# A gated recurrence on one core: blocks of 32 tokens inverted at once on VectorE, the inverse put into keys and values, and one activation table for logarithm and exponential

## The chip, the cores and the metric

The kernel runs on one core of one Trainium2 chip. TensorE (PE in the tables) multiplies matrices, VectorE (DVE), ScalarE (ACT) and GpSimd (POOL) do the elementwise work, SyncE (SP) issues the DMAs. TensorE results land in eight PSUM banks of 128 partitions and 512 fp32 columns. The metric is the device time of one execution in microseconds. A profiled execution shows a trace of its own.

## The reference

Two transformer blocks, one after the other, on 512 tokens of width 1024. The change touches the second block's recurrence (and, through the activation tables, every place that takes a logarithm and then an exponential). Cut to that part:

```python
def rwkv7_mix(p, w_decay_up, w0, a_up, a0, g_up, k_k, k_a, r_k, lnx_g, lnx_b):
    r, k, v, wd, ad, gd = jnp.split(p, c, axis=-1)          # p: token-shifted projections
    w = -jax.nn.softplus(-(w0 + jnp.tanh(wd) @ w_decay_up)) - 0.5
    a = jax.nn.sigmoid(a0 + ad @ a_up)
    g = jax.nn.sigmoid(gd) @ g_up
    kk = (k * k_k) / max(norm(k * k_k), 1e-12)              # per head of 64
    k = k * (1.0 + (a - 1.0) * k_a)
    decay = jnp.exp(-jnp.exp(w))
    def step(state, inp):                                    # one token, 8 heads, state 64x64
        r_t, d_t, k_t, v_t, kk_t, a_t = inp
        sa = jnp.einsum('bhij,bhj->bhi', state, -kk_t)
        state = (state * d_t[:, :, None, :]
                 + sa[..., None] * (kk_t * a_t)[:, :, None, :]
                 + v_t[..., None] * k_t[:, :, None, :])
        return state, jnp.einsum('bhij,bhj->bhi', state, r_t)
    ...                                                      # group norm, bonus, gate g
```

The second block then has index attention, two output projections, a feed-forward layer and norms; all of them keep their form. Inputs, outputs and parameters are fp32.

## The kernel before

Activations lie transposed: features on partitions, the 512 tokens along the free axis, in tiles of 128x512 numbered 0 to 49 (`tile(i)`). A weight matrix arrives in panels of 128x2048 (1 MB): SP loads one, ScalarE casts its high part (line 1129, `W<-raw`), GpSimd subtracts to get the low part (line 2133), and TensorE takes three fp32r products for each pair of tiles (lines 389 to 391, `product`). One `project` job is 24 such products with 512 columns. Two panels can be raw and two split at a time. Where a panel is split is decided by the order of the code: each engine's program calls `ahead` or `filled` with a TensorE job, and the splits that this job's end permits are put in front.

Each engine has one queue in the order of its code; semaphores tie them together (`pe_done` counts TensorE jobs, `bankN_read` the reads of a PSUM bank, others are named after what they announce). No planner orders the work.

The second block's recurrence is done in four chunks of 128 tokens (loop over `t`), each as two halves of 64 (`e`), for 8 heads of 64 features; a tile holds two heads, the two halves of its partitions. Names of products: `rm` = decayed beta times kappa, whose strict upper part M is to be inverted (I + M), `rn` = keys times kappa, `rb` and `rk` the same with the receptance (RHO), `vrow`, `brow`, `krow` are transposes, `nv` = `rn` times values.

What happens, in order:

- `project("rkv", ..., 12)` and `project("wag", ..., 2)`: 14 jobs, each read on VectorE by `causal_conv` with two taps (token shift, lines 1584 and 1586).
- Preparation, lines 1982 to 2005 on VectorE, 1432 to 1458 on ScalarE, 2245 to 2249 on GpSimd: low-rank products `wup`, `aup`, `gup` (lines 882, 885, 890), head norms `kkn` and bonus `bon` (line 443), the running sum of the logarithm of the decay (1987), its exponentials (1452 to 1455), the scaled keys.
- For each chunk: `rm` (line 911), then `inverse`: level 0 by a mask (GpSimd line 2173, VectorE line 1596), transposes (454), then five levels of doubling. A level is: mask (POOL 2173), product (467), copy (ACT 1191), two products (476, 482), two subtractions (DVE 1602, 1604). `rn`, `rb`, `rk`, `nv` and the transposes are put between (`RW_BETWEEN`, lines 902 to 911, masks on VectorE line 2012).
- For each half: state times keys (929), plus values (DVE 2027), times the inverse (938), negated copy (ACT 1465), state times receptance (945), state update (954, 955), added and decayed on VectorE (2031, 2033). At a chunk's end the output product (964, 965), added on VectorE (2038).
- Group norm (`gmean`, `gvar`, line 443; ScalarE 1473, 1178, 1181), then the `ai` projections of the index attention.

The first block's recurrence already inverts its 32-token blocks on VectorE, with `unit_inverses` (lines 1746 to 1770): transposes of 32x32 blocks (1751), a copy to PSUM (1754), 30 steps of a product and a subtraction (1760, 1761), and back (1764, 1766).

A norm's root is taken as exp(-0.5 ln x): `rstd` (lines 1163, 1164) and `rstds` (1178, 1181). `logarithm_next` (1168) takes a logarithm of no use ahead of time, so that its table is there.

## Time and profile before

| | |
|---|---|
| median of 3 runs | 2430.56 us (2429.46 to 2431.78) |
| the profiled execution's own time | 2427.37 us |
| its span | 2425.6 us |
| PE / DVE / ACT / POOL busy | 2189.3 / 960.2 / 834.9 / 929.5 us |
| chain that ended last | PE 75%, DVE 17%, ACT 4%, issue 2%, POOL 2%, DMA 1% |

The page's second part cuts the span in 40 slices of 60.6 us (a digit is the busy share in tenths, PEclk the granted TensorE clock):

```profile
PE   6986999999999889999989588889899888999997
DVE  2587449836431332221022843332892552000001
PEclk9997999999999999999999688888899999999999
```

Slices 23 to 27 (counted from 0; 1395 to 1698 us) hold the second recurrence: TensorE is not full and its clock is not fully granted. Slice 22 is the preparation before it.

### The profile page before, as it was taken

How to read it: one execution, taken by the hardware profiler on the slowest of the kernel's cores; microseconds unless marked ns; L12 is line 12 of the kernel's file. 1: busy time of each engine (PE TensorE's matmuls, PEld its weight loads, DVE VectorE, ACT ScalarE, POOL GpSimd, SP SyncE). 2: the span in 40 equal slices, each digit the busy share in tenths (PEclk: the TensorE clock that was granted, in tenths of full speed). 3: DMA queues.
4: the chain of work that ended last, by engine and by line, in shares of the span. 5: the costliest groups of instructions: out<-in, count | busy, mean ns of one | idle time of the engine just before them, and what ended most of it. 6: DMA issues, size and time to landing. Idle time of an engine off the chain costs nothing.

```text
span 2425.6 us, 28119 instructions
## 1 busy us (share of the span) xinstructions
PE 2189.3 (90%) x11186; PEld 1763.6 (73%) x11186; DVE 960.2 (40%) x1520; ACT 834.9 (34%) x1098; POOL 929.5 (38%) x350
## 2 busy tenths in 40 slices
PE   6986999999999889999989588889899888999997
PEld 3674888766778768888867278776687666888886
DVE  2587449836431332221022843332892552000001
ACT  3544243365452233222222411114322553322222
POOL 2433524433124345545534412222133224555453
PEclk9997999999999999999999688888899999999999
DMA  6121124410112322222332000000122121222231
GB/s 266 70 70 35 35 105 180 173 68 35 50 55 88 121 70 104 91 101 102 107 123 103 18 1 1 1 1 35 53 73 101 37 103 70 87 104 87 104 105 69
DMA packets 25328, 194.36 MB, mean 80 GB/s; under 512 B 3056, under 2 KB 3312, under 8 KB 4208
## 3 DMA queue, kind: packets, MB, share of 16 engines
q1 hardware_dynamic: 25200, 192.57, 21.9%
q8 instruction: 90, 1.47, 0.2%
q14 instruction: 38, 0.31, 0.0%
HBM read 188.37 MB, written 4.19 MB: 79 GB/s over the span
## 4 chain that ended last, share of the span: by engine, by line
PE 75%; DVE 17%; ACT 4%; issue 2%; POOL 2%; DMA 1%; DVEq 0%; SPq 0%; ACTq 0%; POOLq 0%
PE ps L389 19%; PE ps L390 19%; PE ps L391 18%; PE ps L443 2%; PE ps L476 2%; DVE st L1623 1%; PE ps L467 1%; DVE ar L2072 1%; PE ps L911 1%; PE ps L482 1%; POOL W L2133 1%; DVE sm L2071 1%; ACT W L1129 1%; PE ps L512 1%; DVE ar L1567 1%
## 5 line engine op out<-in xcount | busy, mean ns | idle before, releaser
L2133 POOL TENSOR_TENSOR W<-raw,W 128x2048 fp32r<-128x2048 f32 x146 | 673.8, 4615 | 1117.4 <-ACT W L1129 1117.0
L389 PE MATMUL ps<-hH,W 128*128 128x512 f32 x1648 | 661.0, 401 | 47.2 <-DVE arR L1578 8.0
L391 PE MATMUL ps<-hH,W 128*128 128x512 f32 x1648 | 646.6, 392 | 0.0
L390 PE MATMUL ps<-arR,W 128*128 128x512 f32 x1392 | 544.3, 391 | 0.0
L1129 ACT CAST W<-raw 128x2048 fp32r<-128x2048 f32 x146 | 278.9, 1910 | 629.3 <-PE ps L391 619.6
L389 PEld LDWEIGHTS ps<-hH,W 128*128 128x128 f32 x1648 | 312.5, 190 | 136.3 <-issue 54.0
L391 PEld LDWEIGHTS ps<-hH,W 128*128 128x128 f32 x1648 | 312.3, 189 | 66.8
L390 PE MATMUL ps<-xL,W 128*128 128x512 f32 x848 | 334.3, 394 | 0.0
L390 PEld LDWEIGHTS ps<-arR,W 128*128 128x128 f32 x1392 | 263.4, 189 | 53.7
L389 PE MATMUL ps<-arR,W 128*128 128x512 f32 x592 | 233.1, 394 | 16.1 <-DVE arR L1552 12.7
L391 PE MATMUL ps<-arR,W 128*128 128x512 f32 x592 | 232.3, 392 | 0.0
L390 PEld LDWEIGHTS ps<-xL,W 128*128 128x128 f32 x848 | 162.1, 191 | 33.1 <-issue 2.2
L389 PEld LDWEIGHTS ps<-arR,W 128*128 128x128 f32 x592 | 112.5, 190 | 41.5 <-DVE arR L1552 8.7
L2173 POOL TENSOR_TENSOR ar<-ar,cm 128x512 f32<-128x512 f32 x48 | 62.5, 1303 | 182.1 <-DVE ar L2019 108.9
L391 PEld LDWEIGHTS ps<-arR,W 128*128 128x128 f32 x592 | 112.1, 189 | 23.6
L443 PE MATMUL ps<-ar,cm 128*128 128x512 f32 x172 | 86.8, 646 | 33.0 <-DVE ar L1996 17.9
L2106 DVE TENSOR_TENSOR ar<-ar,ps 128x512 f32<-128x512 f32 x22 | 15.1, 688 | 220.6 <-PE ps L391 220.6
L1586 DVE SCALAR_TENSOR_TENSOR ar<-ps,cols,ar 128x511 f32<-128x511 f32 (+1 forms) x130 | 97.4, 749 | 4.6
L443 PEld LDWEIGHTS ps<-ar,cm 128*128 128x128 f32 x172 | 33.0, 202 | 77.8 <-issue 58.6
L1584 DVE TENSOR_SCALAR ar<-ps,cols 128x512 f32<-128x512 f32 x46 | 35.9, 779 | 103.7 <-PE ps L391 103.3
L1133 ACT CAST arR<-ar 128x512 fp32r<-128x512 f32 x74 | 46.0, 621 | 79.4 <-DVE ar L2106 29.5
L1602 DVE TENSOR_TENSOR ar<-ar,ps 128x512 f32<-128x512 f32 x40 | 27.5, 688 | 109.9 <-PE ps L482 93.2
(365 smaller groups left out, 2663.6 us busy)
## 6 DMA issues: line engine op xcount, KB each, us to landing
raw<-panels_dram SPq DMA_DIRECT2D x146, 1024.0 KB, 4.7
ar<-ada_dram SPq DMA_DIRECT2D x12, 2048.0 KB, 11.2
xT<-xT_dram SPq DMA_DIRECT2D x2, 2048.0 KB, 7.8
out_dram<-xT SPq DMA_DIRECT2D x1, 2048.0 KB, 7.3
xT<-out_dram SPq DMA_DIRECT2D x1, 2048.0 KB, 7.7
out_dram<-xT SPq DMA_DIRECT2D x4, 512.0 KB, 2.6
cm<-cm_dram SPq DMA_DIRECT2D x1, 1152.0 KB, 31.4
wide<-wide_dram SPq DMA_DIRECT2D x1, 1024.0 KB, 4.7
```

The lines of the kernel that those rows point to most:

```text
L389: mm(out, lhs[0], rhs[0], start=first, stop=False)
L390: mm(out, lhs[0], rhs[1], start=False, stop=False)
L391: return mm(out, lhs[1], rhs[0], start=False, stop=final)
L443: ins = mm(pst(name, i), sel[k] if isinstance(sel, list) else const(sel), sq, start=(k == 0), stop=(k == len(squares) - 1))
L476: ins = mm(heads4((name, "xt", t, lv, hf))[:, h, :], pair(p1, hf)[:, h, :], pair(xtr, hf)[:, h, :], start=True, stop=True)
L1129: link(nc.scalar.copy(W[:, n % SPLIT, 0, :], raw[:, n % RAW, :]), panel_high, n + 1)
L1133: link(nc.scalar.copy(dst, src), done, value)
L1584: link(ts(out, src, taps[-1], bias, ALU.mult, ALU.add if bias is not None else ALU.bypass))
L1586: ins = stt(out[:, j:S], src[:, 0:S - j], taps[n - 1 - j], out[:, j:S], ALU.mult, ALU.add)
L1602: link(tt(pair(xtr, hf), pair(xtr, hf), heads4((name, "xt", t, lv, hf)), ALU.subtract), *read((name, "xt", t, lv, hf)))
L2133: link(tt(W[:, n % SPLIT, 1, :], raw[:, n % RAW, :], W[:, n % SPLIT, 0, :].bitcast(F32), ALU.subtract), panel_low, n + 1)
L2173: link(tt(pair(mk, hf), pair(am, hf), bm(const(f"lvl{lv}")), ALU.mult), s, value)
```

## The change

One rewrite of the second recurrence and one edit of `logarithm_next`.

- The inverse. `rm` is computed for all four chunks first; one `unit_inverses` call on VectorE inverts all 32-token blocks of all heads and chunks (it now takes its tiles as arguments and serves both blocks). The step from 32 to 64 tokens stays on TensorE: `invert_0` (transposes), `invert_1` (p5), `invert_2` (xt5), for chunks 0 and 1 ahead of the loop, for 2 and 3 inside it. ScalarE copies the off-diagonal corners (`corners`), GpSimd clears them.
- Order of the projections: `wag` job 0 and keys first (`RKV_ORDER` = 12, 4..7, 0..3, 8..11, 13); six of the 14 jobs, `bon` and `gup` stand on TensorE beside the VectorE inverse. The panel of `wag` is loaded twice ("gd").
- The loop. The inverse is multiplied into keys (`solved_keys`, `xk`, scaled by the decay on VectorE) and into values (`solved_values`). The state is one 128x512 tile, two heads to a 128x128 block, so that a half is: `solved_state` (four products, added in PSUM to the solved values), a copy on ScalarE (`updates`), `state_update` (four products, added in PSUM to `key_values`), an addition and a decay on VectorE (`state`). Outputs are summed in one bank (`yt`).
- The preparation moves some VectorE products to GpSimd (keys, receptance, bonus) and to ScalarE (`kap`), and drops the scaling of the decay into the activations (`RATE`).
- `logarithm_next` preloads the table set that holds both functions; eight more calls of it stand ahead of groups of such functions.
- The `trig` load waits until the last `yt`. Banks: chain 0 to 3 for u, z and y, work 4 to 7.

```diff
-    for i in range(7):
+    for i in (5, 6):
...
+RW_U, RW_Z, RW_Y, RW_WORK = (0, 1), (2,), (3,), (4, 5, 6, 7)
+RKV_ORDER = (12, *range(4, 8), *range(4), *range(8, 12), 13)
...
-                project("rkv", h_mix, 12, lambda k: norm_step("low", "rms3", k))
-                project("wag", h_mix, 2)
+                project("wag", h_mix, 1, lambda k: norm_step("low", "rms3", k))
+                project("rkv", h_mix, 1, i0=4)
...
+                for t in range(NT):
+                    products("rm", t, ALL_BANKS)
...
+                project("rkv", h_mix, 1, i0=3, banks=CHAIN_BANKS)
+                project("rkv", h_mix, 4, i0=8, banks=CHAIN_BANKS)
+                project("gd", h_mix, 1, i0=1, banks=CHAIN_BANKS)
...
+                def solved_values(t, e):
...
+                        ins = mm(pst(("u", t, e))[eb, h * 64:(h + 1) * 64], pair(RW_AX + 2 * t, h % 2)[:, h // 2, eb], tile(NVT[t])[:, h * 64:(h + 1) * 64],
+                                 start=(h == 0), stop=(t + e == 0 and h == H - 1))
...
+                def solved_state(t, e):
...
+                    for p in range(4):
+                        ins = mm(pst(("u", t, e))[eb, p * P:(p + 1) * P], tile(KAP + p)[:, ec], tile(RW_T)[:, p * P:(p + 1) * P], start=False, stop=(p == 3))
...
+                for t in range(NT):
+                    if t:
+                        solved_state(t, 0)
+                    solved_values(t, 1)
+                    out_values(t)
+                    products("rb", t, RW_WORK)
+                    rows("brow", t, RW_WORK)
+                    if t:
+                        out_state(t, 0)
+                    key_values(t, 0)
+                    state_update(t, 0)
+                    if t + 1 < NT:
+                        products("rk", t + 1, RW_WORK)
+                    if t + 2 < NT:
+                        invert_0(t + 2)
+                    solved_state(t, 1)
+                    if t + 1 < NT:
+                        key_values(t, 1)
+                    out_state(t, 1)
+                    if t + 1 < NT:
+                        rows("krow", t + 1, RW_WORK)
+                    if t + 2 < NT:
+                        invert_1(t + 2)
+                    if t + 1 < NT:
+                        state_update(t, 1)
+                    out_update(t)
+                    if t + 2 < NT:
+                        invert_2(t + 2)
+                    if t + 1 < NT:
+                        solved_keys(t + 1)
+                        solved_values(t + 1, 0)
...
-                link(af(st[:, 60:61], col("one"), ACT.Ln))
+                nc.scalar.preload_act_table_set("natural_log_exp_and_others")
...
+                for k in range(1, 31):
+                    n = 31 - k
+                    product = tile(temporary)[:, 0:n * k].rearrange("p (i j) -> p i j", j=k)
+                    link(tt(product, low3[:, k + 1:32, k:k + 1].to_broadcast([P, n, k]), unit3[:, k:k + 1, 0:k].to_broadcast([P, n, k]), ALU.mult))
+                    link(tt(unit3[:, k + 1:32, 0:k], unit3[:, k + 1:32, 0:k], product, ALU.subtract))
...
+                units = unit_inverses(RW_AX, RW_LOW, RW_PRODUCT, "rw_blocks", "rw_solved")
+                next(units)
+                mix(8)
+                mix(9)
+                for _ in range(5):
+                    next(units)
```

VectorE where the inverse of the first chunk begins, before. Names are line, operation, output<-input, shape; 1596 makes level 0, 1602 and 1604 are a level's subtractions, 2012 a mask of `rn`:

```order
L2019 COPY ar<-ps 128x512 [waits pe_done,rw_state]
L2019 COPY ar<-ps 128x512 [waits pe_done,bank1_read]
L1596 TENSOR_TENSOR ar<-cm,ar 128x512 [waits rw_masked0,bank2_read]
L1596 TENSOR_TENSOR ar<-cm,ar 128x512 [waits rw_masked0,rw_xt0]
L1602 TENSOR_TENSOR ar<-ar,ps 128x512 [waits pe_done,rw_xt0]
L1604 TENSOR_TENSOR ar<-ar,ps 128x512 [waits bank1_read]
L1602 TENSOR_TENSOR ar<-ar,ps 128x512 [waits pe_done,bank2_read]
L1604 TENSOR_TENSOR ar<-ar,ps 128x512 [waits bank3_read]
L2012 TENSOR_TENSOR ar<-ps,cm 128x512 [waits pe_done,bank4_read]
```

The same engine and place in the changed kernel, from the last mask of `rm` (2195) on; 1790 to 1794 open `unit_inverses`, 1777 and 1779 are the token shift of a projection, 1799 and 1800 a step:

```order
L2195 TENSOR_TENSOR ar<-ps,cm 128x512 [waits pe_done,bank1_read]
L1790 STREAM_TRANSPOSE ar<-ar 32x1024 [waits bank2_read]
L1790 STREAM_TRANSPOSE ar<-ar 32x1024 [waits dve_chain] x3
L1793 TENSOR_SCALAR ps<-ar 128x512 [waits pe_done,dve_chain] x2
L1794 MEMSET ps 128x32 [waits dve_chain]
L1777 TENSOR_SCALAR ar<-ps,sm4 128x512 [waits pe_done,dve_chain]
L1779 SCALAR_TENSOR_TENSOR ar<-ps,cols,ar 128x511 [waits dve_chain]
L1777 TENSOR_SCALAR ar<-ps,sm4 128x512 [waits pe_done,bank3_read]
L1779 SCALAR_TENSOR_TENSOR ar<-ps,cols,ar 128x511 [waits dve_chain]
L1799 TENSOR_TENSOR ar<-ar,ps 128x30 [waits bank4_read]
L1800 TENSOR_TENSOR ps<-ps,ar 128x30 [waits dve_chain]
L1799 TENSOR_TENSOR ar<-ar,ps 128x58 [waits dve_chain]
```

What moved: the waits for TensorE and GpSimd inside the inverse are gone; its steps wait for VectorE itself, and projections are read between them.

TensorE in a half, before. 929 is state times keys, 938 the product with the inverse, 945 state times receptance (its second group, one more row, and then the update of lines 954 and 955 follow):

```order
L929 MATMUL ps<-ar 64x64 [waits bank3_read,rw_state]
L929 MATMUL ps<-ar 64x64 x3
L929 MATMUL ps<-ar 64x64 [waits bank4_read]
L929 MATMUL ps<-ar 64x64 x3
L938 MATMUL ps<-ar 64x64 [waits rw_rhs,bank5_read,bank2_read,bank1_read]
L938 MATMUL ps<-ar 64x64 x7
L945 MATMUL ps<-ar 64x64 [waits bank6_read]
```

And in the changed kernel, the second half of the third chunk (`t` = 2, `e` = 1); 991 is `solved_state`, 1000 `key_values`, 1026 `out_state`, 878 the transposes of the next keys, 1008 `state_update`:

```order
L991 MATMUL ps<-ar 64x128 [waits bank5_read,bank2_read]
L991 MATMUL ps<-ar 64x128 x3
L1000 MATMUL ps<-ar 128x128 [waits bank2_read,bank4_read]
L1000 MATMUL ps<-ar 128x128 x3
L1026 MATMUL ps<-ar 128x64 [waits rw_decayed]
L1026 MATMUL ps<-ar 128x64 x3
L878 MATMUL ps<-cm,ar 128x128 [waits bank7_read]
L878 MATMUL ps<-cm,ar 128x128 x3
L1008 MATMUL ps<-trig,ar 128x128 [waits bank4_read,bank1_read]
L1008 MATMUL ps<-trig,ar 128x128 x3
```

Two groups carry the state (991 and 1008) where there were three (929, 938, 954 with 955), VectorE no longer stands between the first and the second (`rw_rhs` is gone), and twelve products that wait for neither group lie between them.

ScalarE at the last norm of the program (`rstd`), before; 1168 is `logarithm_next`, 1163 the logarithm, 1164 the exponential:

```order
L1168 ACT_TABLE_LOAD
L1168 ACTIVATE st<-cols 128x1 [waits norm_squares]
L1163 ACTIVATE ar<-ps,cols 128x512 [waits pe_done,act_chain]
L1164 ACT_TABLE_LOAD
L1164 ACTIVATE ar<-ar 128x512 [waits bank2_read]
```

And in the changed kernel:

```order
L1286 ACT_TABLE_LOAD [waits norm_squares]
L1281 ACTIVATE ar<-ps,cols 128x512 [waits pe_done]
L1282 ACTIVATE ar<-ar 128x512 [waits bank0_read]
```

The table load between the two functions is gone. In the whole program ScalarE's table loads go from 56 to 35.

## Rows read from the trace of the kernel before

**Rows 1.** Busy time by stage: length, instructions, granted clock (PEclk), DMA.
```profile
1257.00:1330.00 73.00, 72.80 (x321) 60.05 (x322) 21.06 (x29) 14.51 (x11) 27.66 (x6) 1.00 0.24 84
1330.00:1387.00 57.00, 26.77 (x58) 11.94 (x56) 50.48 (x55) 28.92 (x43) 26.09 (x15) 0.68 0.06 22
1387.00:1455.00 68.00, 57.38 (x518) 53.53 (x519) 24.91 (x40) 12.01 (x22) 15.89 (x13) 0.83 0.01 1
...
1591.00:1655.00 64.00, 55.84 (x501) 52.05 (x501) 21.57 (x37) 12.01 (x22) 13.12 (x10) 0.83 0.00 1
```
**Rows 2.** Chain that ended last, 1380 to 1660 us: start, length, engine, line.
```profile
1380.81 2.09 PE ps L911 x11
...
1387.03 1.97 PE ps L454 x8
...
1454.67 1.97 PE ps L454 x8
...
1654.94 3.69 PE ps L443 x8
```
**Rows 3.** Groups by line, 1387 to 1655 us: busy us, mean ns, idle before.
```profile
L467 PE MATMUL ps<-ar 128*128 128x128 f32 x320 | 49.5, 306 | 10.6 <-DVE ar L1604 10.6
...
L2012 DVE TENSOR_TENSOR ar<-ps,cm 128x512 f32<-128x512 f32 x24 | 16.6, 692 | 0.8
```
**Rows 4.** Timeline of one half, chunk 2: start, length, operation, idle before.
```profile
1501.11 1.94 PE L938 MATMUL ps<-ar 64*64 64x64 f32 x16 [2.64 <-DVE st L1654]
...
1503.14 0.59 ACT L1465 ACTIVATE ar<-ps 64x512 f32<-64x512 f32 x1 [6.67 <-PE ps L938]
...
1505.92 0.42 DVE L2031 TENSOR_TENSOR ar<-ar,ps 128x256 f32<-128x256 f32 x1 [5.07 <-PE ps L955]
...
1509.17 1.64 PE L938 MATMUL ps<-ar 64*64 64x64 f32 x13 [0.72 <-DVE st L1654]
```
**Rows 5.** Chain of waits, 1460 to 1486 us: small products back to back.
```profile
1462.57 0.89 PE ps L482 x8
...
1484.10 1.73 PE ps L902 x16
```
**Rows 6.** Groups by line, VectorE, whole span: the first block's `unit_inverses`.
```profile
L1761 DVE TENSOR_TENSOR ps<-ps,ar 128x30 f32<-128x30 f32 (+14 forms) x30 | 10.1, 338 | 1.0
...
L1760 DVE TENSOR_TENSOR ar<-ar,ps 128x30 f32<-128x30 f32 (+14 forms) x30 | 9.8, 328 | 1.0
...
L1751 DVE STREAM_TRANSPOSE ar<-ar 32x1024 f32<-32x1024 f32 x4 | 8.2, 2044 | 0.1
...
L1766 DVE STREAM_TRANSPOSE ar<-ar 32x1024 f32<-32x1024 f32 x4 | 7.6, 1911 | 0.1
...
L1764 DVE COPY ar<-ps 128x512 f32<-128x512 f32 x2 | 1.4, 693 | 0.1
```
**Rows 7.** Timeline, preparation: token shift's first operation, an exponential.
```profile
1330.45 0.75 DVE L1584 TENSOR_SCALAR ar<-ps,sm 128x512 f32<-128x512 f32 x1 [3.90 <-PE ps L391]
...
1370.99 0.63 ACT L1452 ACTIVATE ar<-ar 128x512 f32<-128x512 f32 x1 [13.86 <-DVE ar L2002]
```
**Rows 8.** Stretches of 2 us in the halves of chunk 2.
```profile
1500.00:1502.00 2.00, 0.89 (x9) 0.92 (x10) 0.75 (x3) 0.00 (x0) 0.00 (x0) 0.60 0.00 0
...
1518.00:1520.00 2.00, 1.20 (x14) 1.01 (x13) 1.56 (x3) 0.00 (x0) 0.41 (x1) 1.00 0.00 0
```
**Rows 9.** Timeline, preparation: VectorE beside GpSimd.
```profile
1333.47 3.69 DVE L1552 TENSOR_TENSOR narrow<-wix,narrow 128x64 fp32r<-128x64 f32 x1 [1.48 <-ACT narrow L1133]
...
1351.09 1.72 POOL L2245 TENSOR_TENSOR ar<-ar 128x512 f32<-128x512 f32 x1 [14.01 <-DVE ar L1994]
...
1351.72 1.64 DVE L1996 SCALAR_TENSOR_TENSOR ar<-ar,cols 128x512 f32<-128x512 f32 x1
```
**Rows 10.** Chain of waits at the third norm.
```profile
1244.50 1.28 ACT L1164
```
**Rows 11.** Groups by line, ScalarE, whole span.
```profile
L1181 ACT ACT_TABLE_LOAD x11 | 14.1, 1283 | 0.2
```

More of the change, by code:

```diff
@@ L956, in block_2, with rows @@
-                        end(ins)
+                            ins[par] = mm(heads4((what, t, par))[:, p, :], tile(lhs + p)[b, c], tile(rhs + p)[b, c], start=True, stop=True)
+                    for par in range(2):
+                        end(ins[par], ((what, t, par), 0))
+                def rows(what, t, banks):
+                    begin((what, t), banks=banks)
+                    for p in range(4):
+                        ins = turn(heads4((what, t))[:, p, :], tile({"vrow": V2, "brow": BT, "krow": KT, "kaprow": KAP}[what] + p)[:, t * P:(t + 1) * P],
+                                   const("ident"))
+                    end(ins)
@@ new lines, in row @@
+                def row(base, t, h):
+                    return tile(base + h // 2)[:, t * P + 64 * (h % 2):t * P + 64 * (h % 2) + 64]
+                pe.wait_ge(sem("rw_ready"), 4)
+                for t in range(NT):
+                    products("rm", t, ALL_BANKS)
+                for b in range(2):
+                    begin("rw_blocks", b, (DENSE_BANKS[b],))
+                    end(mm(pst("rw_blocks", b)[:, 0:1], const("ident"), const("ones")[:, 0:1], start=True, stop=True))
+                project("rkv", h_mix, 1, i0=3, banks=CHAIN_BANKS)
@@ new lines, in later_values @@
+                def later_values(t):
+                    for par in range(2):
+                        emptied(pe, ("rn", t, par))
+                    emptied(pe, ("vrow", t))
+                    begin(("nv", t), banks=CHAIN_BANKS)
+                    for h in range(H):
+                        ins = mm(pst(("nv", t))[:, h * 64:(h + 1) * 64], pair(NTR[t % 2], h % 2)[:, h // 2, :], row(V2, t, h), start=True, stop=True)
+                    end(ins)
+                pe.wait_ge(sem("kt_ready"), 4)
@@ L1432, in block_2, with in_place @@
+                def in_place(base, t):
+                    return ar[:, base:base + 4, t * P:(t + 1) * P]
+                emptied(act, "wag", 0)
                 link(af(tile(WA)[0:64, :], tile(WA)[0:64, :], ACT.Tanh), sem("lora_act"), 1)
-                act.wait_ge(small2_in, 32)
+                key_parts(0)
+                for p in range(4):
+                    filled(act, "wup", p)
+                    link(af(tile(LD + p), pst("wup", p), ACT.Sigmoid, bias=col("w0", p)), *read("wup", p))
@@ L1440, in block_2 @@
+                logarithm_next()
+                decays(0)
+                decays(1)
+                key_parts(2)
+                decays(2)
+                decays(3)
+                key_parts(3)
                 for p in range(4):
@@ L1997, in block_2 @@
+                for _ in range(3):
+                    next(units)
+                mix(12)
+                for _ in range(3):
+                    next(units)
+                mix(13)
+                for _ in range(3):
+                    next(units)
                 for p in range(4):
```

650 lines of the change are left out of this document (376 added, 274 removed).

## The prediction, as it was put on record before the changed kernel ran

> **What bounds the kernel now.** I read the page's slices first. TensorE is busy to nine tenths nearly everywhere; the exception of length is the second recurrence. The table of stretches by stage [rows 1] shows the order of things: from 1257 to 1330 us TensorE is full at the full clock with 14 projection jobs (321 products in 72.8 us, 0.227 us each, 5.45 us a job of 24). From 1330 to 1387 VectorE is busy 50.5 of 57 us and TensorE 26.8: the preparation is bound by VectorE. Then come four chunks of about 68 us in which TensorE counts as busy 57 us, at a mean granted clock of 0.83.
>
> The chain that ended last gives the borders [rows 2]: first `rm` products at 1380.8, first transposes at 1387.0, those of the second chunk at 1454.7 (the two between repeat at 68 us), group norm at 1654.9. So from 1257.2 to 1654.9 there are 397.7 us, of which the four chunks take 267.9.
>
> Within a chunk the chain goes product, copy, two products, two subtractions, level after level; from the borders and the half below, some 46 us of the 68 are the inverse. The five levels' first product alone is 320 records, 160 products (an fp32 product leaves two) [rows 3]. A half is a chain of its own: product with the inverse at 1501.11, copy 2.03 us later, state addition at 1505.92, next half's product at 1509.17 [rows 4]: 8.06 us a half. So before, waits and dependent products set the length; TensorE's 0.89 us for four 128x128 products, 0.22 each, and 1.73 us for eight with 64 columns, again 0.22 each [rows 5], are the other price.
>
> **The change, part by part.** The old stage from 1257.2 to 1654.9 is replaced by four pieces, each worked out from rows.
>
> *a, to the last mask of `rm`.* TensorE's work up to `rw_ready` is eight jobs (43.6 us) and twelve fp32 products of 512 columns, 0.86 us each (four of 0.22; four in a row took 3.69 with their start [rows 2]): 10.3 us. The first job runs in the shadow of the norm and ends about 1.2 us after 1257.2, so without any wait TensorE is through at 1258.4 + 38.2 + 10.3 = 1307. Then a token shift (two operations of 0.75 and their starts, 1.57 [rows 7]), three multiplications, 32 products of `rm` (7 us; 3.5 if the two halves of the rows work at once), the last masks (0.69 each [rows 3]): 1315 to 1319. That is the lower end. VectorE's own share is about 43 us (eight shifts 12.6, four running sums and differences 8, twelve multiplications, four factors, four decays, four clips and eight masks 23), so it isn't the bound either; the two wait for each other and for ScalarE (16 exponentials at 0.63 [rows 7], Sigmoid, Tanh and table loads at 1.28, all in one queue, where the second `key_parts` waits for a projection before `aup` can be read). Following that queue job by job I come to `rw_ready` at 1316 without disturbance.
>
> What stands against it: VectorE beside GpSimd. A VectorE operation that takes 0.69 us alone took 1.64 while GpSimd multiplied, and a 64-column subtraction took 3.69 under a panel's split [rows 9]. The change puts eight GpSimd multiplications of 1.7 us and about four splits of 4.6 us into this piece. I take 3 us for the rest after the queue's own course and 7 for `rm` and its masks, which follow one another by bank: end at 1326. Upper end 1340, if each of the splits is met.
>
> The Trainium skill ("SBUF — State Buffer", Who interferes with whom) says that a VectorE instruction with two SBUF inputs and a GpSimd instruction that reads SBUF exclude each other for their whole length, and that one with a single SBUF input outside the two-port modes is free. The trace agrees in the 1.64 us row. By that rule alone all 8 x 1.7 + 4 x 4.6 = 32 us of GpSimd could fall on VectorE here, and nothing on the inverse, whose steps read one operand from PSUM. That is the second rival below.
>
> *b, the block inverse.* The first block runs the same code on the same shapes: 10.1 + 9.8 + 8.2 + 7.6 and twice 1.4 for copies [rows 6], and some 67 starts of 0.03: 40.6 us. Beside it in the same queue: six shifts (9.4), four bonus products (2.9), eight masks of `rn` (5.6), a small subtraction (0.3): 58.8. TensorE delivers its six jobs at 5.45 us from 1326 to 1359, which VectorE has to await for some 4 us in all (the gate's job is the last: 1359, shift to 1360.5, and 27 us of steps, masks and the final transposes remain). I take 64, so `rw_solved` at 1390. Ends 59 and 72 (the small subtraction under a split 3.7, low clock in the first jobs). The six jobs, 33 us, that stood ahead of everything now lie beside it and cost nothing.
>
> *c, before the loop.* Inverse steps of chunks 0 and 1, `rk`, `krow`, `xk`, first values: 76 products at 0.22 are 16.7, and TensorE has been idle before, so the first few microseconds run at the half clock, as at 1500 to 1502 [rows 8]. I take 20 (14 to 26): loop begins at 1410.
>
> *d, the loop.* A full chunk has 96 products and transposes (solved state 8, solved values 16, output values 8, `rb` 8, `rk` 8, transposes 8, output state 8, key values 8, update 8, output update 8, keys 8); the first has 88, the last 60, and chunks 0 and 1 carry 24 of the inverse each. That is 112 + 120 + 96 + 60 = 388, against 268 a chunk, 1072 in all, before. At 0.22 each they would be 85 us. About half are 64 wide on one side and go pairwise on the two halves of the array's columns, or load half the weights; the small products of the old half took 1.94 us for eight at a clock of 0.60 [rows 4, 8]. I take 0.173 as the mean: 67 us. The chain is shorter than this: four products 0.9, copy 0.59, four products 0.9, addition in two parts of 0.42 [rows 4], 0.4 of handing over: 3.7 us a half, 30 for eight. So the loop is bound by TensorE's order. For waits at bank turns, the unhidden last chunk and a clock that falls now and then I add 11: 78 us. Ends 66 and 92. `gmean` then starts at 1488 to 1489, against 1654.9.
>
> Pieces: 1654.9 - 1488.9 = 166.0 us saved.
>
> *Tables.* On the chain between logarithm and exponential stands a load of 1.28 us [rows 10]. It goes at four norms (5.1 us; the first norm waits for DMA anyway), at the latent norm (1.3), in the head norms of the attention (two loads in one queue, 2) and at the group norm (1.3). Of the eleven loads of line 1181 [rows 11] most are hidden by TensorE's work and give nothing. I take 10, between 6 and 15. The Tanh load that is new lies in piece a.
>
> The Trainium skill ("ScalarE: Activation LUTs", What ACT_TABLE_LOAD costs) gives about 2.66 us for each switch of set, load and drain together. The rows here show 1.28 and an exponential that starts 0.02 us later; by the page the edit would give some 20 us instead of 10.
>
> *At nothing:* the second load of the `wag` panel (one cast and one split beside VectorE's inverse), the later `trig` load (its first reader comes after five projections of 5.45 us), fewer constants. If their cover were gone, the panel would cost 1.9 + 4.6 us.
>
> **Sum.** The profiled execution's own time is 2427.4 us. 2427.4 - 166.0 - 10.0 = 2251.4. The median of the runs lies 3.2 us above the profiled one, so 2254.6, rounded 2255.
>
> **The rivals.**
>
> *The loop at the half clock.* For it: in the halves of the old chunk the granted clock is 0.60 and below from 1500 on, with TensorE in work, and comes back only by 1518 to 1520 [rows 8]. Against it: there are pauses of 1 to 3 us in the old half, and the new order has few. The price is the 67 us of products once more, less the waits that they cover: +60, 2315. Partly so (a third of it) is within my range.
>
> *The preparation stretched by GpSimd.* Price: the rest of the 32 us above what I took, about +22: 2277. For it the rows of 3.69 and 1.64 us; against it, most VectorE work there reads PSUM or falls between splits.
>
> *By the page's price of a table,* some 10 us less: 2245.
>
> *The loads don't go:* the preload is made and the loads between the functions stay. Against it, the order of ScalarE shows 35 instead of 56 loads. Then 2265.
>
> *Slower than before.* One mechanism: VectorE's 60 dependent small operations of the inverse wait for the port each time that GpSimd works. To eat the 176 us each would have to lose 2.9 us. The first block's same 60 operations have 338 and 328 ns means [rows 6] beside the first block's splits, so there was next to no such wait. It would decide only if GpSimd's new work lay on all of it. Time then 2435.
>
> **How the numbers follow.** Chances: the forecast 0.68, half clock 0.12, stretched preparation 0.11, the page's tables 0.04, loads stay 0.03, slower 0.02. The forecast's own ends: low, 10 for a, 5 for b, 6 for c, 12 for d, 4 for tables, which don't fall together: about -30; high, 14, 8, 6, 14 and 4, and part of the two slower rivals: +37. Range 2225 to 2292. About 0.2%, 5 us, is what a measurement of this kernel can tell. Nothing but the last rival and an error of 170 us leads to a slower kernel: faster 0.97, same 0.01, slower 0.02.
>
> **What the profile of the changed kernel would show.** `rm` masks end 69 us after the first projections' 1257; `unit_inverses` opens then and its last transposes end 64 us later, with VectorE busy over nine tenths and TensorE idle for the last 20; about 20 us to the first solved values, 78 from there to the group norm. The last chunk's chain is a half of some 4 to 5 us. Exponentials follow logarithms without a load. I am wrong if the loop takes over 95 us at full clock, which would say that bank turns or VectorE's queue bind it and not TensorE; if PEclk is near 0.5 through it (first rival); if VectorE's 0.7 us operations show 3 us and more in the preparation (second); or if anything after the recurrence starts to wait for a panel.

## The result, and the profile after

The changed kernel takes 2255.18 us (median of 4 runs, 2254.23 to 2256.45) against 2430.01 (2424.17 to 2431.78) in the same session: ratio 0.9282, 95% interval 0.9271 to 0.9293. The forecast was 2255. Its profiled execution took 2255.01 us with a span of 2253.2. The sum was right and its terms were not: three of them were off by 9, 12 and 13 us.

The page after, its second part (40 slices of 56.3 us; busy share in tenths, PEclk the granted clock):

```profile
PE   6996799999999988999999868998998888999998
DVE  2589555866443033222200697438925442000001
PEclk9998899999999999999999989998999999999999
```

Of the six slices with PEclk 6 or 8 from the preparation to the end of the recurrence one is left, slice 23, and the dip of TensorE stands there too (1296 to 1352 us): the preparation, where VectorE shows 9.

The stretches by stage, cut at the borders that the prediction named (length, PE, PEld, DVE, ACT, POOL busy with counts, granted clock, DMA share, GB/s). They answer to [rows 1]:

```profile
1256.33:1316.00 59.67, 53.75 (x201) 38.17 (x201) 42.49 (x41) 37.51 (x49) 30.19 (x12) 0.94 0.14 53
1316.00:1330.40 14.40, 0.13 (x1) 0.00 (x0) 14.04 (x10) 1.95 (x3) 11.14 (x7) 0.63 0.20 73
1330.40:1338.40 8.00, 7.72 (x76) 7.21 (x77) 5.53 (x8) 0.22 (x1) 0.00 (x0) 0.81 0.01 2
1338.40:1394.50 56.10, 53.71 (x313) 42.79 (x311) 48.99 (x95) 20.68 (x26) 24.25 (x14) 1.00 0.16 57
1394.50:1401.70 7.20, 0.01 (x1) 0.00 (x1) 7.04 (x4) 0.59 (x1) 0.00 (x0) 0.76 0.00 0
1401.70:1416.70 15.00, 15.00 (x150) 14.49 (x152) 5.06 (x8) 7.36 (x14) 1.22 (x4) 0.89 0.00 1
1416.70:1434.70 18.00, 18.00 (x198) 16.43 (x194) 7.95 (x14) 4.79 (x9) 0.00 (x0) 1.00 0.01 2
1434.70:1454.80 20.10, 20.10 (x226) 18.62 (x225) 8.03 (x15) 5.26 (x9) 0.00 (x0) 1.00 0.01 2
1454.80:1470.20 15.40, 15.26 (x188) 14.12 (x185) 6.69 (x13) 2.92 (x5) 0.00 (x0) 1.00 0.01 1
1470.20:1482.30 12.10, 10.00 (x117) 8.96 (x115) 3.04 (x6) 2.33 (x4) 0.00 (x0) 1.00 0.01 4
```

Read with the prediction's pieces. Piece a is the first three rows, piece b the next two, c the sixth, d the last four.

| piece | predicted | measured |
|---|---|---|
| a, to the last mask of `rm` | 69 (58 to 83) | 82.1 (1256.3 to 1338.4) |
| b, block inverse | 64 (59 to 72) | 63.3 |
| c, before the loop | 20 (14 to 26) | 15.0 |
| d, the loop | 78 (66 to 92) | 65.6 |
| sum, against 397.7 before | 231 | 226.0 |
| all else (tables), from the spans | -10 (-6 to -15) | -0.7 (172.4 in all, less 171.7) |

The errors are +13, -1, -5, -12 and +9, and cancel to 3.6 us: the profiled execution was forecast at 2251.4 and took 2255.0. (The forecast's pieces were added as 1488.9 less 1257.2, 231.7.) The median came within 0.6 us of 2254.6 by a further accident: before the change the profiled execution lay 3.2 us under the median, after it 0.2.

Of the 171.7 us, 47.7 were saved up to the point where the inverse begins (129.8 before, 82.1 after, six of the 14 projections having moved behind it) and 124.0 in inverse and chunks together (267.9 before, 143.9 after). No run separates what the inverse on VectorE brings from what the new order of the loop brings; the 124.0 us are the sum of both.

Three rows show the state of things. In the second row TensorE stands still for 14.3 us while VectorE is full (14.0 of 14.4 us). In the seventh and eighth TensorE is busy for the whole of both chunks. In the tenth, the last chunk, it waits for 2.1 us. Fifteen of the table loads that are left stand in front of a group of logarithms and exponentials; their row answers to [rows 11] (35 loads in all, 56 before):

```profile
L1286 ACT ACT_TABLE_LOAD x15 | 19.2, 1283 | 0.3
```

The late preparation is seen in the timeline of VectorE and GpSimd from 1311 us on (start, length). It answers to [rows 9]:

```profile
1312.37 0.69 DVE L2187 TENSOR_TENSOR ar<-ar 128x512 f32<-128x512 f32 x1
1313.10 4.94 DVE L2188 TENSOR_TENSOR ar<-ar 128x512 f32<-128x512 f32 x1
1318.08 1.63 DVE L2189 TENSOR_TENSOR ar<-ar 128x512 f32<-128x512 f32 x1
1319.74 1.63 DVE L2187 TENSOR_TENSOR ar<-ar 128x512 f32<-128x512 f32 x1
```

```profile
1312.83 4.66 POOL L2384 TENSOR_TENSOR W<-raw,W 128x2048 fp32r<-128x2048 f32 x1 [3.17 <-ACT W L1247]
1317.57 1.59 POOL L2488 TENSOR_TENSOR ar<-ar 128x512 f32<-128x512 f32 x1
1319.24 1.59 POOL L2490 TENSOR_TENSOR ar<-ar 128x512 f32<-128x512 f32 x1
```

The same multiplication takes 0.69 us alone, 1.63 beside a GpSimd multiplication, and 4.94 where a panel's split has just begun: it ends 0.55 us behind the split (1312.83 + 4.66 = 1317.49; 1318.04). The twelve multiplications ahead of `rw_ready` (lines 2187 to 2189) take 21.1 us together instead of 8.3. Earlier in the same piece, at 1276.8, one of the four differences behind the running sums (line 2170, 0.69 alone, both operands in SBUF as well) took 4.9 us beside the split of 1275.7.

The inverse, in contrast, has four splits beside it, three of them on its 60 small steps, and shows none of that. Groups by line, VectorE, 1338 to 1402 us (busy us, mean ns, idle before), to be laid beside [rows 6]:

```profile
L1800 DVE TENSOR_TENSOR ps<-ps,ar 128x30 f32<-128x30 f32 (+14 forms) x30 | 10.1, 338 | 1.0
L1799 DVE TENSOR_TENSOR ar<-ar,ps 128x30 f32<-128x30 f32 (+14 forms) x30 | 9.8, 328 | 1.0
L1790 DVE STREAM_TRANSPOSE ar<-ar 32x1024 f32<-32x1024 f32 x4 | 8.1, 2026 | 0.1
...
L2195 DVE TENSOR_TENSOR ar<-ps,cm 128x512 f32<-128x512 f32 x8 | 5.5, 692 | 0.8 <-PE ps L870 0.6
```

338 and 328 ns, the first block's means to the nanosecond.

### The profile page after: what moved, and what is told of

Its sections match the earlier page's. It is cut to its first block, busy times and chain, and to the rows that moved or that the text cites. A ratio compares the mean times of both kernels' runs of the same rounds, so it can differ in the third digit from the quotient of the medians.

```text
span 2253.2 us, 25853 instructions
## 1 busy us (share of the span) xinstructions
PE 2056.8 (91%) x10214; PEld 1639.8 (73%) x10214; DVE 952.8 (42%) x1493; ACT 798.2 (35%) x1049; POOL 883.3 (39%) x319
## 4 chain that ended last, share of the span: by engine, by line
PE 74%; DVE 17%; ACT 5%; issue 2%; POOL 2%; DMA 1%; SPq 0%; ACTq 0%; DVEq 0%; POOLq 0%
PE ps L397 20%; PE ps L399 19%; PE ps L398 19%; PE ps L451 2%; DVE st L1826 1%; DVE ar L2323 1%; DVE sm L2322 1%; ACT W L1247 1%; DVE ar L1760 1%; POOL W L2384 1%; PE ps L481 1%; DVE ar L1779 1%; DVE arR L1745 1%; DVE ar L1906 1%; PE ps L816 1%
## 5 line engine op out<-in xcount | busy, mean ns | idle before, releaser
L397 PE MATMUL ps<-arR,W 128*128 128x512 f32 x592 | 232.6, 393 | 16.1 <-DVE arR L1745 12.8
L2357 DVE TENSOR_TENSOR ar<-ar,ps 128x512 f32<-128x512 f32 x22 | 15.1, 688 | 220.6 <-PE ps L399 220.6
L1879 DVE SCALAR_TENSOR_TENSOR ar<-ar,st 128x512 f32<-128x512 f32 x56 | 61.0, 1090 | 2.0
L1311 ACT ACTIVATE ar<-ar,st 128x128 f32<-128x128 f32 (+3 forms) x64 | 36.0, 563 | 55.4 <-DVE st L1826 54.2
```

Of the source, the lines that this page charges most:

```text
L397: mm(out, lhs[0], rhs[0], start=first, stop=False)
L1311: ins = af(tile(smt[i])[:, 0:w], tile(smt[i])[:, 0:w], ACT.Exp, bias=st[:, i:i + 1], scale=scale, accum_out=st[:, 4 + i:5 + i])
L1879: ins = stt(acc, tile(ADA_BASE[i] + k), st[:, k:k + 1], acc, ALU.mult, ALU.add)
```

## The experiments

Each version was timed together with the kernel before. Differences are to the changed kernel's 2255.2 (ratio 0.9282), unless said otherwise; a ratio's interval is about 0.0013 to either side, so 3 us on the time. The kernel before had medians of 2430.0 beside the changed kernel and of 2429.4, 2427.0 and 2428.3 beside the three groups of experiments. So a difference taken from the ratios can be 1 to 2 us off the one taken from the times; where that matters both are given. Lengths of pieces come from the profiled execution of each version, which differs from its median by up to 3.3 us; they are compared with the changed kernel's profiled execution (2255.0).

### The tables alone, and the tables undone

```diff
             def logarithm_next():
-                link(af(st[:, 60:61], col("one"), ACT.Ln))
+                nc.scalar.preload_act_table_set("natural_log_exp_and_others")
```

in the kernel before, with the same calls ahead of the groups:

> The kernel before with nothing but the table edit: the dummy logarithm becomes the load of the one table, and it is loaded ahead of every group of logarithms and exponentials (33 loads instead of 56). Theory A, the prediction's term: 10 us less than before (6 to 15), 2420, ratio 0.996. Theory B, read from the traces of before and after by aligning TensorE's instructions outside the recurrence: a norm gives 0.4 to 0.5 us and not 1.3, because VectorE's first multiplication comes earlier and falls beside a GpSimd split (3.34 us for three instead of 2.33); the latent norm gives 1.9, the group norm 1.3, and stretches at the half clock give part of it back: 2 to 5 us less in all, 2426, ratio 0.9985.

Measured: 2425.35 us (11 runs) against 2429.4, ratio 0.9983 [0.9974, 0.9992]: 4.1 us less, as theory B had it. And the reverse, in the changed kernel:

> The changed kernel with the old tables everywhere but in the preparation of the recurrence (56 loads instead of 35; the recurrence itself is untouched). Theory A (the table term is 10 us, and something else gave time back elsewhere): 10 us more than the changed kernel, 2265, ratio to before 0.932. Theory B (the term is 2 to 5 us): 2257 to 2260, ratio 0.929 to 0.930. The pieces of the recurrence keep their lengths under both (82, 63, 15 and 66 us).

Measured: 2264.05 us, ratio 0.9317 [0.9304, 0.9330]: 8.9 us more. Neither theory as I wrote it: the time is near A's, but the pieces did not keep their lengths. The profiled execution (2261.99, the shortest of four) is 7.0 us longer than the changed kernel's. In it a was 1.3 us longer, b 66.5 instead of 63.3 and c 15.6, so 4.8 us of the 7.0 lie in pieces whose tables were left alone. Against that, two stretches at the half clock that the changed kernel has at 1627 and 1774 us are not there, 1.9 and 1.6 us. That leaves 5.7 us for everything else, the loads among it, which is between the two theories. In b, VectorE waits for TensorE's `rn` products where it did not before. The masks' row there, kernel with the old tables:

```profile
L2188 DVE TENSOR_TENSOR ar<-ps,cm 128x512 f32<-128x512 f32 x9 | 6.2, 692 | 4.1 <-PE ps L870 3.9
```

TensorE's granted clock was 0.55 and 0.59 from 1384 to 1392 us in that kernel and 1.00 in the changed one, where the same instructions in the same order come 2.2 us earlier. So the half clock falls in other places in the two kernels, and a single such place is worth 3 us in b. That the shift brings it is not shown.

Where the single loads went is seen at the third norm. ScalarE, VectorE and GpSimd in the changed kernel:

```profile
1241.89 1.28 ACT L1286 ACT_TABLE_LOAD   x1
1243.19 0.69 ACT L1281 ACTIVATE ar<-ps,cols 128x512 f32<-128x512 f32 x1
1243.90 0.63 ACT L1282 ACTIVATE ar<-ar 128x512 f32<-128x512 f32 x1
```

```profile
1244.64 3.34 DVE L1760 SCALAR_TENSOR_TENSOR ar<-xT,cols,ar 128x512 f32<-128x512 f32 x3 [4.14 <-ACT ar L1282]
```

```profile
1241.35 4.50 POOL L2384 TENSOR_TENSOR W<-raw,W 128x2048 fp32r<-128x2048 f32 x1 [3.54 <-ACT W L1247]
```

The load of [rows 10] between logarithm and exponential is gone, and ScalarE is through 1.9 us earlier (0.4 of which it had already). But VectorE's first multiplication now starts at 1244.64, inside a split that lasts until 1245.85, and three of them take 3.34 us where each takes 0.75 alone. TensorE starts at 1248.85 instead of 1249.73: of the gain at this norm 0.5 us is left, and likewise at the second and fourth. The last norm of the program has no split beside it and gains 1.5: from the last TensorE product to the end are 13.0 us before and 11.5 after.

### GpSimd later

```diff
+            pool.wait_ge(sem("rw_ready"), 4)
             ahead(pool, ("rm", 0, 0))
             for p in range(4):
```

> The changed kernel, but GpSimd waits for rw_ready before its split and its eight multiplications (L2488, L2490) that ran beside VectorE's twelve multiplications of two SBUF operands. Theory A (these collide: the twelve took 21 us in all and take 0.69 each, 8.3, when alone; three of them stay beside other GpSimd work): the preparation is 9 to 11 us shorter, first rm products near 1320 instead of 1330.4, and the block inverse, which now has the eight multiplications and the split beside it, keeps its 63 us because its steps read one operand from PSUM. Time 2245, ratio to before 0.924. Theory B (the inverse suffers as well from GpSimd): the inverse grows by up to 17 us, time 2255 to 2262. Theory C (the twelve were slow for another reason): no change, 2255.

Measured: 2250.14 us, ratio 0.9261 [0.9246, 0.9276]. The twelve multiplications took 11.2 us, `rm` began at 1320.6, and a was 9.5 us shorter: theory A for the preparation, and with it three quarters of the error of a. GpSimd's work moved onto the masks and the inverse: five of the eight multiplications and four splits lie in b, three splits on the 60 small steps. These, and the masks:

```profile
L1800 DVE TENSOR_TENSOR ps<-ps,ar 128x30 f32<-128x30 f32 (+14 forms) x30 | 10.1, 338 | 1.0
L1799 DVE TENSOR_TENSOR ar<-ar,ps 128x30 f32<-128x30 f32 (+14 forms) x30 | 9.8, 328 | 1.0
...
L2195 DVE TENSOR_TENSOR ar<-ps,cm 128x512 f32<-128x512 f32 x9 | 6.2, 692 | 6.8 <-PE ps L870 6.5
```

The steps are unchanged to the nanosecond, so theory B falls. Yet b grew from 63.3 to 69.8, and its third row says why: VectorE waited 6.5 us for TensorE's `rn`. The clock was at half there; this kernel in 20 us of b, and the changed one in the 11 us with the same instructions (x110 and x111):

```profile
1374.00:1394.00 20.00, 20.00 (x110) 18.89 (x109) 12.68 (x26) 5.28 (x9) 0.00 (x0) 0.51 0.00 1
```

```profile
1383.00:1394.00 11.00, 11.00 (x111) 10.42 (x111) 9.64 (x24) 5.28 (x9) 0.00 (x0) 1.00 0.01 1
```

TensorE had waited 1.84 us (changed kernel, at 1382) and 1.85 us (this one, at 1373) just ahead of this, for the same instruction.

### Taking the wait away

In the changed kernel, ScalarE's corner copies behind the first copies of values:

```diff
-                act.wait_ge(sem("mk_zero"), 1)
-                corners(0)
-                corners(1)
...
                 copied(tile(NVT[0]), ("nv", 0))
+                act.wait_ge(sem("mk_zero"), 1)
+                corners(0)
+                corners(1)
```

> The changed kernel, but ScalarE copies the corners of chunks 0 and 1 (1.7 us) behind the first rows of V and the first later values instead of ahead of them, so that TensorE's wait of 1.84 us ahead of the first later values (L910) goes. Theory A (VectorE binds the block inverse): b stays at 62.5 to 63.3, 2254 to 2255. Theory B (TensorE's wait is passed on to VectorE): b is 1.8 us shorter, 2253.

Measured: 2252.31 us, ratio 0.9278 [0.9265, 0.9291]; b was 63.0. The ratio is that of the changed kernel within its interval. The edit did not do what it was meant to: of TensorE's wait of 1.84 us ahead of L910, 1.55 remained, now for VectorE's mask (L2195) instead of ScalarE. So neither theory was tested; that VectorE binds b rests on its 56.0 us busy of 63.3 (rows four and five of the table of stretches). The span is 2.9 us shorter than the changed kernel's, and not in the recurrence (233.3 instead of 233.5 us from the norm to `gmean`): two short stretches at the half clock in the index part, at 1627 and 1774 us, did not occur (1.7 and 1.6 us). 1626 to 1630 us, changed kernel, then this one:

```profile
1626.00:1630.00 4.00, 4.00 (x13) 3.14 (x12) 3.80 (x7) 0.00 (x0) 0.00 (x0) 0.62 0.47 195
```

```profile
1626.00:1630.00 4.00, 4.00 (x19) 3.29 (x18) 3.80 (x7) 0.00 (x0) 0.00 (x0) 1.00 0.50 207
```

The same projections, TensorE busy throughout in both, 13 products against 19, and the two kernels' instructions only 0.2 us apart just ahead of there. Both edits together:

> GpSimd after rw_ready (as in the run that gained 5 us) and the corners later, together. In the former the preparation was 9.5 us shorter, but b grew by 6.5 us, in which TensorE ran at the half clock from 1374 to 1404 after the same wait of 1.85 us that the changed kernel passes at full clock. Theory A (the wait brings the half clock): without it the clock stays, b is 63 again, 2244, ratio 0.9235. Theory B (the wait is too short to matter; the half clock comes with any such stretch of small products): b stays near 70, 2250.

Measured: 2246.19 us, ratio 0.9247 [0.9234, 0.9260]. This is a version faster than the changed kernel, by 0.4%: its interval lies clear of the changed one's, which that of GpSimd alone does not. a 72.7, b 65.2: nearer to A. Here too 1.55 us of the wait remain, for VectorE's mask, and the clock was at half for 3 to 4 us after it and not for 27:

```profile
1374.00:1394.00 20.00, 12.81 (x110) 11.93 (x110) 16.77 (x26) 7.46 (x14) 1.21 (x4) 0.84 0.00 1
```

So 0.3 us less of waiting went with 24 us less of the half clock right behind it. The test that theory A asked for, a kernel without the wait, was not made, and what decides is open.

### Keeping TensorE at work ahead of the loop

```diff
-                    for h in range(H):
-                        ins = mm(pst(("nv", t))...
+                    for _ in range(5 if t == NT - 1 else 1):
+                        for h in range(H):
+                            ins = mm(pst(("nv", t))...
```

> The changed kernel with the last product group ahead of rw_solved (nv of chunk 3, eight products of 0.24 us) issued five times with the same result, so that TensorE works until about 1402 instead of falling idle at 1394.5. Theory A (the idle 7 us bring the half clock of 1396 to 1408, under which c runs): the clock stays at 1.00 and c takes 10 to 11 us instead of 15, time 2251. Theory B (c is bound by its chain of products, copies and subtractions): c stays at 14 to 15.

Measured: 2257.85 us, ratio 0.9302 [0.9289, 0.9314]. The clock stayed at 1.00 and c took 13.6 us: 1.4 shorter, not 4 to 5, so theory A was right on the clock and wrong on its price: most of c is the products themselves. More than that, 2.6 us, was lost in the last chunk:

```profile
1472.00:1486.60 14.60, 12.46 (x116) 11.09 (x114) 2.91 (x5) 2.33 (x4) 0.00 (x0) 0.76 0.03 4
```

where the changed kernel has its last chunk, 12.1 us, at 1.00. And the kernel had come to the norm 2.8 us late, half-clock stretches at 438 and 513 us among the causes, far ahead of the edit. In the combined version, with three instead of five:

> The same, and the later values of chunk 3 issued three times with the same result (3.8 us more of products that nobody waits for), to shorten TensorE's idle stretch ahead of rw_solved from 7 to about 3 us. Theory A: the clock stays at 1.00 into c, which is 1.5 us shorter (13.5), 2242 to 2243. Theory B: no change against the kernel without them, or the half clock turns up later instead, as in the run with five times, where it fell on the last chunk.

Measured: 2246.86 us, ratio 0.9253 [0.9240, 0.9266], c 15.3 with the clock at 0.50 from 1392 to 1396: no change, theory B.

### What the loop is bound by

```diff
                         if n:
+                            link(tt(diagonal(tile(RW_T)), diagonal(tile(RW_TD)), diagonal(pst(("rz", t, e))), ALU.add))
                             ins = tt(diagonal(tile(RW_T)), diagonal(tile(RW_TD)), diagonal(pst(("rz", t, e))), ALU.add)
```

> The changed kernel with the state addition (two operations of 0.42 us on VectorE, seven halves) made twice over with the same result: the chain of the loop is 0.9 us longer a half, 6.2 us in all; TensorE's work is the same. Theory A (chunks 0 to 2 are bound by TensorE's order: 53.4 us busy of 53.5): only the last chunk, where TensorE waits 2.1 of 12.1 us, shows it: 1 to 2 us more, loop 67 instead of 65.6. Theory B (the chain binds): 5 to 6 us more, loop 71 to 72, 2261.

Measured: 2258.87 us, 3.7 more (5.6 by the ratios), ratio 0.9305 [0.9292, 0.9317], d 70.7. That number alone would speak for B. The stretches (the four chunks, kernel with the longer chain) speak for A:

```profile
1415.90:1433.90 18.00, 18.00 (x197) 16.43 (x194) 8.81 (x16) 4.76 (x9) 0.00 (x0) 1.00 0.01 2
1433.90:1454.00 20.10, 20.07 (x226) 18.53 (x224) 9.61 (x19) 5.25 (x9) 0.00 (x0) 1.00 0.01 2
1454.00:1469.60 15.60, 14.56 (x176) 13.43 (x174) 7.08 (x15) 2.92 (x5) 0.00 (x0) 1.00 0.01 2
1469.60:1486.60 17.00, 13.58 (x131) 12.08 (x129) 5.21 (x10) 2.33 (x4) 0.00 (x0) 0.79 0.02 3
```

Chunks 0 and 1 keep 18.0 and 20.1 us with 0.9 us more in each half's chain, chunk 2 takes 0.2 more. All the rest, 4.9 us, is in chunk 3, where the changed kernel already waited: its last half begins 2.3 us later in the chunk, and then the half clock over the last products (0.79 in the mean) takes 2.6.

```diff
-                    for p in range(4):
-                        for par in range(2):
+                    for par in range(2):
+                        for p in range(4):
```

> The changed kernel, but the K=64 products rm, rn, rk and rb are issued four of the lower rows and then four of the upper rows, as before, instead of in turn. Theory A (products on the two halves of the rows run at once, which is why 8 of them show 1.09 us, 0.136 each, in the loop and not 1.73): rb and rk (64 products) cost some 0.08 us more each, 5.4 us, of which the loop shows most, and rm 2 to 3 us more ahead of the masks: 2260 to 2263. Theory B (they are short for another reason, as loading only 64 rows, or the loop is bound by its chain): within 1 us of 2255.

Measured: 2263.61 us, ratio 0.9316 [0.9303, 0.9329], 8.4 us more. In the loop d is 69.3, 3.7 more, and one group carries it. Changed kernel, then this one, TensorE, 1416 to 1488 us:

```profile
L870 PE MATMUL ps<-ar 64*128 64x128 f32 x112 | 8.5, 282 | 0.0
```

```profile
L870 PE MATMUL ps<-ar 64*128 64x128 f32 x112 | 11.7, 282 | 0.0
```

56 products (two records each) take 0.152 us apiece in turn and 0.209 apart, and 282 ns is the mean length of a record in both: they overlap in the one and not in the other. Theory A, with 0.06 us for each instead of 0.08. a was 1.1 us longer, b 1.7, c 0.8, so the recurrence is 7.2 us longer (in the profiled execution, which is 6.4 us longer in all, the shortest of four). The other half of the question, results on the two halves of the output rows:

```diff
-                    for h in range(H):
+                    for h in (0, 2, 4, 6, 1, 3, 5, 7):
```

in three loops, those of L968, L1018 and L1035:

> The changed kernel, but output values, output update and solved keys (L1018, L1035, L968; 96 products with M=64 whose results go in turn to the lower and the upper 64 output rows) are issued as four of one half and then four of the other. Theory A, as the prediction put it: they go pairwise on the two halves of the array's columns, 0.13 to 0.16 us each and 0.22 when apart: 0.07 us x 96 = 7 us more, of which 6 in the loop, 2262. Theory B: they are short because only 64 columns of weights are loaded (L978, whose eight results go to one half, shows 0.12 us each as well): within 1.5 us of the changed kernel.

Measured: 2261.45 us, ratio 0.9314 [0.9302, 0.9327], 6.3 more (7.8 by the ratios). The recurrence was 4.1 us longer, all of it from the first solved values to `gmean`; the other 2.3 us of the profiled execution lie outside the recurrence, where nothing was edited. Of the three groups, here the output values and half of the output updates, changed kernel and then this one (products leave two records each):

```profile
L1018 PE MATMUL ps<-ar 128*64 128x128 f32 x64 | 5.1, 276 | 0.0
...
L1035 PE MATMUL ps<-ar,trig 128*64 128x128 f32 x32 | 2.2, 279 | 0.0
```

```profile
L1018 PE MATMUL ps<-ar 128*64 128x128 f32 x64 | 6.3, 279 | 0.0
...
L1035 PE MATMUL ps<-ar,trig 128*64 128x128 f32 x32 | 3.2, 279 | 0.0
```

From 0.14 to 0.20 us a product at L1035, from 0.16 to 0.20 at L1018: theory A, at two thirds of its size. What theory B was built on, L978 (64 columns on both sides, results in one half of the output rows), stays at 0.13 to 0.14, and why it is short without such a turn was not tested.

The Trainium skill ("TensorE: Matmul & The Clock Gate", Part 3: Packing small matmuls, The mechanism) says that products which fill only part of the array run at the same time when they sit on different parts of it. The trace agrees for both directions, 0.152 against 0.209 and 0.14 against 0.20 us.

### The projections ahead

```diff
+                project("rkv", h_mix, 1, i0=3)
+                project("rkv", h_mix, 4, i0=8)
+                project("gd", h_mix, 1, i0=1)
                 pe.wait_ge(sem("rw_ready"), 4)
...
+                for j in range(8, 14):
+                    mix(j)
                 dve.wait_ge(sem("kt_ready"), 4)
```

> The changed kernel with the six projection jobs put back ahead of rm (and their token shifts ahead of the masks). Theory A (what the prediction says of the six jobs: 33 us that stood ahead and now cost nothing): a comes out 33 us longer and b 9.4 shorter by the six shifts, 23 us more, 2278. Theory B: TensorE sat idle 14.3 us ahead of rm for VectorE, so the jobs stand there only 18 us too long, and b gets the six shifts (9.4) and the 3.4 us of waits for them back: about 5 us more, 2260.

Measured: 2259.74 us, ratio 0.9306 [0.9294, 0.9319]: 4.6 us more (5.8 by the ratios), theory B. a grew by 17.8 us and b fell from 63.3 to 51.4, 6.4 us more for the whole recurrence. Laying 33 us of TensorE work beside the inverse saved some 5 us and not 33, since TensorE had 14.3 us to wait in any case and VectorE has its six shifts to do on either side of the border.

## Why the prediction was right, point by point

**Right: what is replaced by what.** From 1256.3 to `gmean` the stage took 226.0 us instead of 397.7, 171.7 saved where 166.0 were predicted. The five levels of [rows 3] and the halves of 8.06 us of [rows 4] are gone. One half's chain in the last chunk, from the timeline of the changed kernel (state update, state addition, `solved_state`, copy):

```profile
1476.00 1.05 PE L1008 MATMUL ps<-wide,ar 64*128 64x128 f32 x8
1477.16 0.87 DVE L2265 TENSOR_TENSOR ar<-ar,ps 64x256 f32<-64x256 f32 x2 [1.99 <-PE ps L1008]
...
1478.08 1.09 PE L991 MATMUL ps<-ar 128*64 128x128 f32 x8 [1.03 <-DVE ar L2265]
...
1479.26 0.58 ACT L1642 COPY wide<-ps 64x512 f32<-64x512 f32 x1 [4.35 <-PE ps L991]
```

From 1476.00 to 1479.84 it is 3.8 us, where 3.7 were predicted. Of the terms put at nothing, the later `trig` load held: from the end of the group norm to 1620 us TensorE's instructions stay 173.9 us ahead of the same instructions in the kernel before, so nothing was waited for in addition.

**Piece a, 13 us too short: the term for GpSimd was mis-sized.** I took 3 us for "the rest after the queue's own course"; the twelve multiplications alone lost 12.8 (21.1 less 8.3), one difference of line 2170 another 4.2, and with GpSimd held back from the last nine multiplications 9.5 of the 13 came back. `rm` and its masks took 8.0 us where 7 were predicted. The price stood in [rows 9], 1.64 us for 0.69, and GpSimd's 32 us were counted. What I did not do is to lay the two queues beside each other: the twelve multiplications of two SBUF operands stand at the end of the piece (1305 to 1330 us, one token shift each ahead of the fourth and the tenth), exactly when GpSimd has two splits and eight multiplications. The second rival put it at +22 over the forecast; it was there with 13. That the total still met the forecast is luck: the other errors hid it.

The rule of the Trainium skill that I had set against the trace ("SBUF — State Buffer", Who interferes with whom) is borne out on both sides here: two SBUF operands, 1.63 and 4.94 us for 0.69; one operand from PSUM, 338 and 328 ns with three splits beside them.

**Piece b, right** (63.3 for 64), for the reasons given: VectorE is busy 56.0 of 63.3 us. TensorE is idle for the last 7 and not for the last 20. Its length holds only at the full clock, since the `rn` products stand between: 66.5 and 69.8 us in two kernels where the half clock fell on them.

**Piece c, 5 us too long.** 76 products at 0.22 gave 16.7; at full clock it takes 13.6, and `rk`, the keys and the values, which go in pairs, are among them. The half clock cost 1.4, where I had added 3.3 for it.

**Piece d, 12 us too long: the 11 us for waits and clock were not needed.** The products' own time was right: 63.4 us busy (18.0 + 20.1 + 15.3 + 10.0) for 388 products, 0.163 each where I took 0.173. Waits were 2.2 us, all but 0.1 in the last chunk, and the clock was 1.00. The mechanism, TensorE's order and not the chain, is shown for three chunks by the longer chain that cost chunks 0 and 1 nothing and chunk 2 0.2 us; in the last chunk, where TensorE waits, the chain counts as well. The first rival, the loop at the half clock, did not come in any version but for the last 7 us of two.

**Tables, 9 us too much.** The edit gave 4.1 us in the kernel before. The step that failed is the term itself: a load of 1.28 us at four norms was counted in full (5.1), and 2 us for the head norms of the attention. TensorE's instructions laid side by side, before and after, show what came instead: 0.5 us at three of the norms, because VectorE then starts inside a split, and 1.5 at the last; 1.8 at the latent norm and 1.3 at the group norm, where 1.3 was counted for each; nothing at the head norms. That is 6.1 us. The span outside the recurrence is nevertheless only 0.7 shorter, since the changed kernel is 1.6 us late by 540 us (why is open), and loses 2.0 and 1.6 us around its two stretches at the half clock, at 1627 and 1774 us. The latter two did not occur in the run with the corners moved nor in the one with the old tables, which is why I call them a matter of phase and not of this edit. The rival by the Trainium skill ("ScalarE: Activation LUTs", What ACT_TABLE_LOAD costs), about 2.66 us for each switch and by that, as my estimate, some 20 us in all, is further off: 4.1 us measured in the kernel before.

So what is replaced by what, and TensorE's order as the bound of the loop, were foreseen. The 2255 itself was luck: errors of 13, 5, 12 and 9 us have both signs. Its range of 67 us is what such terms deserve.

## What to carry to other kernels

Before GpSimd is given work "for free", lay its queue beside VectorE's in time: here operations with two SBUF operands took 1.63 and 4.94 us for 0.69, those that read PSUM nothing more, and a dense block of the first kind right ahead of TensorE's wait cost 12.8 us. Small products should be issued so that neighbours use different halves of rows or of columns, which was worth 8 and 6 us here by order alone, 7 and 4 us in the recurrence itself. And a term that only shortens another engine's chain by 1 us should be followed to the next shared thing (a split, a clock stretch) before it is counted.

## What was not expected of the hardware

Where the half clock (1.2 instead of 2.4 GHz) falls changes between kernels that issue the same TensorE instructions. The same 110 of them took 11 us at a granted clock of 1.00 in one kernel and 20 at 0.51 in another, where they came 9 us earlier, after the same wait of 1.85 us. Projections with no pause at all had 4 us at 0.62 in one and at 1.00 in another, with the instructions 0.2 us apart. In these kernels a short stretch is worth 1.6 us and the longest 6.5, more than the table edit. What decides it is open.

Of the one kernel with GpSimd held back, the four runs lie at 2246.3, 2247.1, 2253.2 and 2253.4 us, and the profile shows one of the two longer ones; the 6.5 us in b that it shows may be the difference, which I did not test.
